# Sixteen products of constant tiles at the head of TensorE's program, in a 25,892-instruction kernel of two transformer-like blocks

## The chip, the cores and the metric

The kernel runs on one core of one Trainium2 chip. The metric is the device time of the kernel in microseconds (us), the median of the runs. Lower is better. A share of 0.2% is 3.1 us here.

## The reference, cut to what matters

Two blocks follow one another on a sequence of 512 rows of 1024 numbers in fp32. All that matters here is how the first one begins:

```python
def rms_norm(x, g, eps=1e-6):
    xf = x.astype(jnp.float32)
    y = xf * lax.rsqrt(jnp.mean(xf * xf, axis=-1, keepdims=True) + eps)
    return (y * g.astype(jnp.float32)).astype(x.dtype)
...
        h = rms_norm(x, norm_g[l])
...
            h @ w_in[l], IN_SPLITS, axis=-1)
        y_conv = conformer_conv_branch(c_glu, c_gate, conv_dw[l], conv_dw_b[l],
```

The rows are normed, multiplied by a gain, and then by `w_in` (1024 x 11264). The first branch takes 2048 of its columns, `a` and `b`, forms `a * sigmoid(b)`, and runs a causal convolution of 31 taps over the rows, channel by channel. Differential attention, cross attention to a memory of 256 rows, an output product, and a second block (gated mixing, a recurrent mixer, a feed-forward part) come after it.

## The kernel before, in words

The program of each engine is written out by hand, in order, and engines wait for each other on counted semaphores. TensorE (`pe_program`, line 1007) does everything in products of 128x128 stationary tiles. Every fp32 weight and activation is split in two fp32r parts, high and low, and each product of them is three instructions (`mm3`, lines 643 to 645: high x high, low x high, high x low). Weights come in units of 128x1024 numbers (512 KB). SyncE issues one DMA per unit into a ring of four slots (`raw`, line 751), ScalarE writes the high part (line 691), and VectorE or GpSimd the low part (line 699). The split parts have a ring of three places.

The start of the kernel, in order:

- GpSimd (`pool_program`, lines 763 to 778) sets the constants: `ident` to zero and then, as the last of them, to the identity matrix; `ones_all` to one. That last instruction (line 777) raises the semaphore `consts`. TensorE's program begins with a wait for it (line 1008).
- SyncE loads the input rows, four tiles of 128x1024 (`x_in`, line 736), the columns of gains, and then the weight units.
- ScalarE and VectorE share the sums of squares (lines 655 and 2404) and roots of the four tiles, and VectorE scales the rows (`x_in`, line 2409).
- TensorE transposes the scaled rows (`pe_turn_group`, then `pe_turn_pair`, line 979): for each of the 8 groups k of 128 features, two transposes of 128x128 for row tiles 0 and 1 (g = 0), later two for row tiles 2 and 3 (g = 1). The destinations are seven places in the matmul banks 4, 5, 6, 7, 3, 1, 2 (`row_places`), so the eighth group (k = 7) waits until the first place has been read.
- ScalarE reads each transposed group with the gain as the high part `h_T_hi` (line 654), VectorE then forms the low part `h_T_lo` (line 2390). Between those, ScalarE and VectorE split the first weight unit.
- `pe_first_unit` (line 986) computes the first unit, channel tile 0 of `b` (`conv_b` 0). It mixes the transposes of row tiles 2 and 3 with the products of rows 0 to 255, and ends with the products of rows 256 to 511, all of them with 256 moving columns. The unit has 48 instructions of `mm3`.
- `pe_conv_tile` then runs the `a` tile 0 (`conv_a` 0, 24 instructions with 512 moving columns), gate and merge units, and so on for eight tiles. When `conv_a` 0 is done, VectorE multiplies it (line 2387) and starts the taps (lines 2469 and 2390): 31 instructions per tile, back to back, into banks 4 and 5.

Bank 0 is the first place of the ring `units` (banks 0, 1, 2) and receives `conv_b` 0. TensorE works strictly in order, and `conv_b` 0 begins with an instruction that overwrites.

```python
    def pe_turn_pair(pe, what, tiles, g, pair):
...
            for n in range(2):
                if k == 0:
                    pe.wait_ge(*row_ready.at(what, 2 * g + n))
                done = pe.transpose(turned_bank(what, g, k)[:, cut(n)], tiles[2 * g + n][:, cut(k)], ident[:, :])
```

Of the kernel before, what the change touches and what calls it, by code (L numbers as in the profile page):

```python
# [14 lines left out]
P = 128  # L15
# [57 lines left out]
           "d_gate": 6144, "xq": 7168, "x_gate": 8192, "merge": 9216}  # L73
GATE_OF = {0: 0, 1: 2, 2: 1}

KEY_PAIRS = {4: ((0, 0), (0, 1)), 5: ((0, 2), (0, 3)), 7: ((1, 0), (1, 1), (1, 2), (1, 3))}


# [5 lines left out]
def unit_plan():  # L84
# [4 lines left out]
    def f(label, array, column):  # L89
        plan.append((label, array, "F", 0, column))  # L90
# [18 lines left out]
    for n in range(KT):  # L109
        f(("conv_b", n), "w_in", W_IN_AT["conv_b"] + n * P)  # L110
        f(("conv_a", n), "w_in", W_IN_AT["conv_a"] + n * P)
        for half, pair in KEY_PAIRS.get(n, ()):
            plan.append((("xk", half, pair), "w_mem_kv", "T", 256 * pair, half * 512))
# [175 lines left out]
def build(nc, dram, out):  # L289
# [40 lines left out]
    ident = usable("ident", [P, P])  # L330
    ones_all = usable("ones_all", [P, P])
# [142 lines left out]
    banks = [nc.alloc_psum_tensor(f"bank{n}", [P, 512], FP32) for n in range(8)]  # L474
# [495 lines left out]
    def pe_turn_pair(pe, what, tiles, g, pair):  # L970

        for k in (2 * pair, 2 * pair + 1):
            if k == 2 * pair or turned_last(what, k - 1) != k:
                last = turned_last(what, k)
                turn_places(what).take(pe, (what, g, last), turned_lo, what, g, last)
# [4 lines that stand above are left out]
            done.then_inc(*turned.up(what, g, k))  # L980

    def pe_turn_group(pe, what, tiles, g):
        for pair in range(KT // 2):
            pe_turn_pair(pe, what, tiles, g, pair)

    def pe_first_unit(pe, label):


        bank, (hi, lo) = unit_bank(pe, label), parts[turn_of[index[label]]]

        def products(g, k):
            tokens = turned_columns(g)
            pe.wait_ge(*turned_lo.at("x", g, k))
            return mm3(pe, bank[:, tokens], (hi[:, cut(k)], lo[:, cut(k)]), (h_T[0][:, k, tokens], h_T[1][:, k, tokens]),
                       k == 0, k == KT - 1)

        for pair in range(KT // 2):
            pe_turn_pair(pe, "x", x_in, 1, pair)
            if pair == 0:
                pe.wait_ge(*lo_ready(index[label]))  # L1000
            for k in (2 * pair, 2 * pair + 1):
                products(0, k)
        for k in range(KT):
            done = products(1, k)
        done.then_inc(*product.up(*label))

    def pe_program(pe):
        pe.wait_ge(*consts.at())
        pe_turn_group(pe, "x", x_in, 0)
        pe_first_unit(pe, ("conv_b", 0))  # L1010
        key_banks = [[], []]
        for n in range(KT):
            pe_conv_tile(pe, n, key_banks)
        pe_values(pe)
        pe_cross(pe)
        pe_differential(pe)
        pe_first_out(pe)
        pe_second_in(pe)
        pe_rwkv(pe)
        pe_second_out(pe)  # L1020
        pe_ffn(pe)
# [37 lines left out]
    def pe_conv_tile(pe, n, key_banks):  # L1059


        def mean():
            if n == 5:
                pe_conv_mean(pe, 3)

        if n:
            feature_unit(pe, ("conv_b", n), unit_bank(pe, ("conv_b", n)), h_T)
        feature_unit(pe, ("conv_a", n), unit_bank(pe, ("conv_a", n)), h_T)
        if n == 3:
            pe_turn_pair(pe, "mem", mem_in, 0, 2)  # L1070
        if n == 6:
            pe_key_turn(pe, 0)
        for half, pair in KEY_PAIRS.get(n, ()):
            pe.wait_ge(*turned_lo.at("mem", 0, 2 * pair + 1))
            pe_key_pair(pe, half, pair, key_banks[half])
        feature_unit(pe, ("conv_gate", n), unit_bank(pe, ("conv_gate", n)), h_T)
        if n in (1, 2):
            pe_turn_pair(pe, "mem", mem_in, 0, n - 1)
        feature_unit(pe, ("merge", 0, n), unit_bank(pe, ("merge", 0, n)), h_T, mid=mean)
        if n == 3:  # L1080
            pe_turn_pair(pe, "mem", mem_in, 0, 3)
        if n == KT - 1:
            pe_key_turn(pe, 1)

    def pe_values(pe):
        pe.wait_ge(*conv_done.at(KT - 2))
        for half in range(2):
            out_banks = []
            for pair in range(KT // 2):
                token_unit(pe, ("xv", half), pair, out_banks, mem_T, lambda t: value_places.take(pe, ("xv", half, t), v_lo, "x", half, t))  # L1090
                if half == 1 and pair == 1:
                    pe_conv_mean(pe, KT - 1)
                if half == 1 and pair == 2:
                    pe_conv_total(pe, "mean", stats["mean"]).then_inc(*conv_mean.up())
# [197 lines left out]
    def pe_first_out(pe):  # L1292
        for half in range(2):
            places = side if half == 0 else half_places
            out_banks = []
            for pair in range(KT // 2) if half == 0 else (0,):
                if half == 0:
                    pe.wait_ge(*y_lo.at(2 * pair + 1))
                token_unit(pe, ("w_out", half), pair, out_banks, h_T, lambda t: places.take(pe, ("w_out", half, t), row_ready, "x1", t, half))
        token_rows(pe, ("w_out", 1), out_banks, h_T, lambda: pe_turn_group(pe, "emb", x_rows, 0))  # L1300

    def pe_second_in(pe):
        first_units(pe, "emb", EARLY[0:2], h2_T)
        for n in range(2, 4):
            feature_unit(pe, ("pu", n), unit_bank(pe, ("pu", n)), h2_T)
        out_banks = []
        for pair in range(KT // 2):
            token_unit(pe, ("pv", 0), pair, out_banks, h2_T, lambda t: side.take(pe, ("pv", t), sg_gelu, t))
        head = head_features(lambda f: pe_features(pe, f), lambda f: pe_tokens(pe, f))
        for i, n in enumerate(SHIFT_ORDER):  # L1310
            feature_unit(pe, ("rwkv", n), units.take(pe, ("rwkv", n), shift_done, n), h2_T)
            if 2 <= i < 2 + TT:
                t = i - 2
                bank = side.take(pe, ("sg", t), sg_out, t)
                if t == 0:
                    pe.wait_ge(*wsp_lo.at())
                pe.wait_ge(*sg_lo.at(t))
                for g in range(4):
                    done = mm3(pe, bank[:, cut(g)], (v_sg[0][:, cut(g)], v_sg[1][:, cut(g)]),
                               (w_sp[0][:, cut(g)], w_sp[1][:, cut(g)]), True, True)  # L1320
                done.then_inc(*sg_mixed.up(t))
            head_steps(head, i, PE_HEAD_STEPS)
# [237 lines left out]
    def pe_rwkv(pe):  # L1560
        pe.wait_ge(*masks_ready.at())
        pe.wait_ge(*ident_ready.at(1))
        rwkv_rounds(lambda f: pe_features(pe, f), lambda f: pe_tokens(pe, f), lambda f: pe_chunks(pe, f),
                    lambda f: pe_states(pe, f), lambda: pe_out_steps(pe), lambda v: pe_gate_rows(pe, v))
# [21 lines left out]
    def pe_second_out(pe):  # L1586
        pe.wait_ge(*yb_lo.at(FW - 1))
        token_unit(pe, ("w_out_2", 0), KT // 2 - 1, first_out, (Mix(0), Mix(1)), None)
        out_banks = []
        token_unit(pe, ("w_out_2", 1), 0, out_banks, (Mix(0), Mix(1)),  # L1590
                   lambda t: half_places.take(pe, ("w_out_2", 1, t), moved, "mix", t, 1))
        token_rows(pe, ("w_out_2", 1), out_banks, (Mix(0), Mix(1)), lambda: pe_turn_group(pe, "ln1", x_rows, 0))
# [123 lines left out]
    def act_program(act):  # L1716
# [12 lines left out]
        for n in range(KT - 1):  # L1729
# [5 lines left out]
            if n == 6:  # L1735
                act_key_hi(act, 0)
            feed_hi(act, len(KEY_PAIRS.get(n, ())))
            if n == 5:
# [41 lines left out]
    def act_key_hi(act, half):  # L1780
        for h in (2 * half, 2 * half + 1):
            act.wait_ge(*key_turned.at(h))
            for c in range(2):
                activate(act, k_x[0][:, 2 * h + c, :], key_turned_bank(h, c), ACT.Copy, scale=column("x_kn_g", c)).then_inc(
                    *norm_hi.up("xk", h, c))
# [5 lines left out]
    def act_keys(act):  # L1791
# [25 lines left out]
        act_take(act, ("conv_b", n), conv_gate_ring.take(act, n, taken["dve"], "conv_a", n), ACT.Sigmoid)  # L1817
        feed_hi(act, 1 + len(KEY_PAIRS[n]))
        act_key_squares(act, 1)
# [1531 lines left out]
```

## Time and profile before

| what | value |
|---|---|
| three runs | 1571.91, 1572.81, 1574.12 us (median 1572.81) |
| the profiled execution | 1572.88 us |
| its span, first to last instruction | 1570.8 us |
| TensorE busy | 1518.1 us, 97% of the span |
| VectorE busy | 1093.5 us, 70% |
| ScalarE busy | 749.5 us, 48% |
| GpSimd busy | 191.9 us, 12% |
| mean granted TensorE clock, share of full | 0.995 |
| DMA | 166.18 MB, mean 106 GB/s |

The profiled execution lies 2.1 us above its span; that is what surrounds the first and the last instruction. In the timeline of the trace a row has the start (us from the first instruction), the length, the engine, the line of the code, the operation, the tiles, the shape and the count, and in brackets the idle time before it with what ended it. In the row of a group the length runs from the start of the first to the end of the last. The records of TensorE's instructions overlap: the rate of a stream is read from the distance between starts, and the length of one includes filling and emptying the array. PEld is TensorE's loading of stationary tiles.

### The profile page before, as it was taken

How to read it: one execution, taken by the hardware profiler on the slowest of the kernel's cores; microseconds unless marked ns; L12 is line 12 of the kernel's file. 1: busy time of each engine (PE TensorE's matmuls, PEld its weight loads, DVE VectorE, ACT ScalarE, POOL GpSimd, SP SyncE). 2: the span in 40 equal slices, each digit the busy share in tenths (PEclk: the TensorE clock that was granted, in tenths of full speed). 3: DMA queues.
4: the chain of work that ended last, by engine and by line, in shares of the span. 5: the costliest groups of instructions: out<-in, count | busy, mean ns of one | idle time of the engine just before them, and what ended most of it. 6: DMA issues, size and time to landing. Idle time of an engine off the chain costs nothing.

```text
span 1570.8 us, 25892 instructions
## 1 busy us (share of the span) xinstructions
PE 1518.1 (97%) x10408; PEld 1252.6 (80%) x10408; DVE 1093.5 (70%) x1898; ACT 749.5 (48%) x1253; POOL 191.9 (12%) x159
## 2 busy tenths in 40 slices
PE   7999999999999999999999999988898999999998
PEld 6878786888888877777788888767767899989886
DVE  5999994666655478758544747886547978867556
ACT  5544455535522477747632625654424544444223
POOL 2435364500010000000004000000000000000000
PEclk9999999999999999999999999999999999999999
DMA  6323243454465323232424232210002233433331
GB/s 220 94 86 120 90 147 108 160 165 146 147 184 182 116 86 95 90 111 81 147 95 142 74 121 81 81 43 4 3 29 86 90 108 106 123 97 121 101 98 54
DMA packets 45798, 166.18 MB, mean 106 GB/s; under 512 B 5280, under 2 KB 5408, under 8 KB 45680
## 3 DMA queue, kind: packets, MB, share of 16 engines
q1 hardware_dynamic: 43056, 155.95, 30.8%
q0 software_dynamic: 2624, 8.59, 1.9%
q8 instruction: 83, 1.36, 0.4%
q14 instruction: 35, 0.29, 0.1%
HBM read 162.42 MB, written 2.10 MB: 105 GB/s over the span
## 4 chain that ended last, share of the span: by engine, by line
PE 79%; DVE 15%; ACT 3%; issue 2%; DMA 0%; SPq 0%; DVEq 0%; ACTq 0%
PE bank L643 24%; PE bank L645 24%; PE bank L644 23%; DVE bank L2390 7%; PE bank L1366 1%; PE bank L1218 1%; ACT scratch L654 1%; DVE small L2416 1%; DVE x_rows L2390 1%; PE bank L1197 1%; DVE scratch L2387 0%; DVE weight_lo L699 0%; PE bank L1463 0%; ACT weight_hi L691 0%; DMA x_in<-in_x 0%
## 5 line engine op out<-in xcount | busy, mean ns | idle before, releaser
L691 ACT ACTIVATE weight_hi<-raw 128x1024 fp32r<-128x1024 f32 x195 | 205.8, 1057 | 384.6 <-PE bank L645 381.1
L643 PE MATMUL bank<-h_T_hi,weight_hi 128*128 128x512 f32 (+1 forms) x848 | 342.0, 403 | 2.8 <-DVE conv_in L2387 2.1
L699 DVE TENSOR_TENSOR weight_lo<-raw,weight_hi 128x1024 fp32r<-128x1024 f32 x138 | 168.8, 1224 | 238.6 <-ACT weight_hi L691 238.6
L645 PE MATMUL bank<-h_T_hi,weight_lo 128*128 128x512 f32 (+1 forms) x848 | 329.8, 389 | 0.0
L644 PE MATMUL bank<-h_T_lo,weight_hi 128*128 128x512 f32 (+1 forms) x848 | 329.2, 388 | 0.0
L643 PEld LDWEIGHTS bank<-h_T_hi,weight_hi 128*128 128x128 f32 x848 | 160.1, 189 | 43.2 <-issue 8.5
L2390 DVE SCALAR_TENSOR_TENSOR bank<-conv_in,columns,bank 128x512 f32<-128x512 f32 x240 | 181.4, 756 | 8.3
L644 PEld LDWEIGHTS bank<-h_T_lo,weight_hi 128*128 128x128 f32 x848 | 160.3, 189 | 33.5 <-issue 3.6
L645 PEld LDWEIGHTS bank<-h_T_hi,weight_lo 128*128 128x128 f32 x848 | 159.8, 188 | 33.8
L699 POOL TENSOR_TENSOR weight_lo<-raw,weight_hi 128x1024 fp32r<-128x1024 f32 x57 | 141.8, 2488 | 154.1 <-ACT weight_hi L691 154.1
L643 PE MATMUL bank<-h_T_hi,half_weight_hi 128*128 128x256 f32 (+1 forms) x240 | 79.1, 330 | 0.0
L644 PE MATMUL bank<-h_T_lo,half_weight_hi 128*128 128x256 f32 (+1 forms) x240 | 79.1, 330 | 0.0
L645 PE MATMUL bank<-h_T_hi,half_weight_lo 128*128 128x256 f32 (+1 forms) x240 | 79.1, 330 | 0.0
L643 PE MATMUL bank<-branch_hi,weight_hi 128*128 128x512 f32 x192 | 75.8, 395 | 0.1
L645 PE MATMUL bank<-branch_hi,weight_lo 128*128 128x512 f32 x192 | 74.8, 389 | 0.0
L644 PE MATMUL bank<-branch_lo,weight_hi 128*128 128x512 f32 x192 | 74.7, 389 | 0.0
L643 PE MATMUL bank<-weight_hi,hidden_hi 128*128 128x512 f32 x176 | 68.5, 389 | 0.0
L644 PE MATMUL bank<-weight_lo,hidden_hi 128*128 128x512 f32 x176 | 68.5, 389 | 0.0
L645 PE MATMUL bank<-weight_hi,hidden_rest 128*128 128x512 f32 x176 | 68.5, 389 | 0.0
L643 PE MATMUL bank<-weight_hi,h_T_hi 128*128 128x512 f32 x160 | 62.5, 390 | 0.0
L645 PE MATMUL bank<-weight_hi,h_T_lo 128*128 128x512 f32 x160 | 62.3, 389 | 0.0
L644 PE MATMUL bank<-weight_lo,h_T_hi 128*128 128x512 f32 x160 | 62.3, 389 | 0.0
(500 smaller groups left out, 3193.0 us busy)
## 6 DMA issues: line engine op xcount, KB each, us to landing
raw<-in_weights SPq DMA_DIRECT2D x289, 512.0 KB, 3.5
x_in<-in_x SPq DMA_DIRECT2D x4, 512.0 KB, 5.8
x_rows<-in_x POOLq DMA_DIRECT2D x4, 512.0 KB, 4.9
out<-x_rows SPq DMA_DIRECT2D x3, 512.0 KB, 2.6
mem_in<-in_mem POOLq DMA_DIRECT2D x2, 512.0 KB, 4.2
ln_rows<-in_ln_g POOLq DMA_DIRECT2D x4, 256.0 KB, 4.4
ln_rows<-in_ln_b POOLq DMA_DIRECT2D x4, 256.0 KB, 5.1
silu_row<-in_c POOLq DMA_DIRECT2D x1, 512.0 KB, 6.6
```

The source lines that it names most:

```text
L643: pe.matmul(o, lhs[0], rhs[0], start=start, stop=False, skip_group_check=onto)
L644: pe.matmul(o, lhs[0], rhs[1], start=False, stop=False, skip_group_check=onto)
L645: return pe.matmul(o, lhs[1], rhs[0], start=False, stop=stop, skip_group_check=onto)
L654: return act.activation(o, i, func, bias=bias, scale=scale)
L691: act.activation(weight_parts(u)[0][:, :], raw[u % RAW][:, :], ACT.Copy).then_inc(*weight_hi.up(u))
L699: engine.tensor_tensor(lo[:, :], raw[u % RAW][:, :], view(hi[:, :]), ALU.subtract).then_inc(*ready.up(u))
L1197: done = pe.transpose(bank[:, cut(j)], s_ring["s", h, t, 0][:, cut(j)], ident[:, :])
L1218: pe.matmul(bank, ones_head[:, :], norm_ring_d[what, h], start=True, stop=True).then_inc(*norm_sum.up(what, h))
L1366: return pe.matmul(bank[lanes, cut(m, CHUNK)], lhs(m, rows), rhs(m, rows), start=True, stop=True)
L2390: return dve.scalar_tensor_tensor(out=o, in0=a, scalar=scalar, in1=b, op0=op0, op1=op1)
L2416: dve.bn_stats(found[:, 6 * n:6 * n + 6], source[:, cut(n, 512)]).then_inc(*dve_own.up())
```

## The change

TensorE's program gets sixteen products between its wait for the constants and the first transpose. Each multiplies `ones_all` (128x128 ones, stationary) with `ident` (128 moving columns), both plain fp32, into the first 128 columns of bank 0, and each overwrites the one before. No result is read, and no semaphore is raised or waited for.

```diff
+EARLY_PRODUCTS = 16
...
     def pe_program(pe):
         pe.wait_ge(*consts.at())
+        for n in range(EARLY_PRODUCTS):
+            pe.matmul(banks[0][:, 0:P], ones_all[:, :], ident[:, :], start=True, stop=True)
         pe_turn_group(pe, "x", x_in, 0)
         pe_first_unit(pe, ("conv_b", 0))
```

## Rows read from the trace of the kernel before

**Rows 1.** The page: span, busy time by engine, chain that ended last by engine.
```profile
span 1570.8 us, 25892 instructions
...
PE 1518.1 (97%) x10408; PEld 1252.6 (80%) x10408; DVE 1093.5 (70%) x1898; ACT 749.5 (48%) x1253; POOL 191.9 (12%) x159
...
PE 79%; DVE 15%; ACT 3%; issue 2%; DMA 0%; SPq 0%; DVEq 0%; ACTq 0%
```

**Rows 2.** Timeline of all engines, 0 to 16 us.
```profile
2.34 0.28 POOL L777 TENSOR_SCALAR_AFFINE_SELECT ident<-ident 128x128 f32<-128x128 f32 x1 [0.24 <-POOL ones_head L775]
...
8.20 1.43 DVE L2409 TENSOR_SCALAR x_in<-x_in,small 128x1024 f32<-128x1024 f32 x2
...
9.09 3.63 PE L979 MATMUL bank<-ident,x_in 128*128 128x128 f32 x14 [9.09 <-DVE x_in L2409]
...
12.40 3.01 ACT L654 ACTIVATE h_T_hi<-bank,columns 128x256 fp32r<-128x256 f32 x8
...
13.53 1.54 PE L979 MATMUL bank<-ident,x_in 128*128 128x128 f32 x6 [0.81 <-DVE h_T_lo L2390]
...
14.56 1.22 DVE L699 TENSOR_TENSOR weight_lo<-raw,weight_hi 128x1024 fp32r<-128x1024 f32 x1
...
15.83 0.58 PE L643 MATMUL bank<-h_T_hi,weight_hi 128*128 128x256 f32 x1 [0.76 <-DVE weight_lo L699]
```

**Rows 3.** Timeline of TensorE, 17 to 26 us.
```profile
17.28 1.05 PE L979 MATMUL bank<-ident,x_in 128*128 128x128 f32 x4
17.98 0.56 PE L643 MATMUL bank<-h_T_hi,weight_hi 128*128 128x256 f32 x1
18.34 0.41 PE L644 MATMUL bank<-h_T_lo,weight_hi 128*128 128x256 f32 x1
18.56 0.41 PE L645 MATMUL bank<-h_T_hi,weight_lo 128*128 128x256 f32 x1
...
20.12 0.53 PE L643 MATMUL bank<-h_T_hi,weight_hi 128*128 128x256 f32 x1
20.48 0.28 PE L644 MATMUL bank<-h_T_lo,weight_hi 128*128 128x256 f32 x1
20.60 0.28 PE L645 MATMUL bank<-h_T_hi,weight_lo 128*128 128x256 f32 x1
...
25.11 0.40 PE L643 MATMUL bank<-h_T_hi,weight_hi 128*128 128x512 f32 x1
```

**Rows 4.** Waits of VectorE (25 to 245 us) and TensorE (20 to 260): total, times, longest.
```profile
DVE conv_in L2387 <- PE bank L645: 6.3, 1, 6.3
...
PE bank L1028 <- ACT conv_out L1789: 3.3, 1, 3.3
```

**Rows 5.** A plain fp32 product with ones: timeline near 634 us, and line 1213 (min/median/max ns).
```profile
633.88 1.02 PE L1213 MATMUL bank<-scratch,ones_all 128*128 128x512 f32 x2
...
L1213 PE MATMUL bank<-scratch,ones_all x16: 591/592/697, 583.2 to 781.9; 128*128 128x512 f32 x16
```

**Rows 6.** Timeline of TensorE: transposes near 880 us, and from 1213 to 1219 us.
```profile
880.05 1.86 PE L979 MATMUL bank<-ident,x_rows 128*128 128x128 f32 x15 [0.83 <-DVE x_rows L2427]
...
1213.53 0.27 PE L979 MATMUL bank<-ident,x_rows 128*128 128x128 f32 x1
1215.96 1.78 PE L979 MATMUL bank<-ident,x_rows 128*128 128x128 f32 x11 [2.16 <-DVE x_rows L2427]
1218.20 0.66 PE L979 MATMUL bank<-ident,x_rows 128*128 128x128 f32 x4 [0.47 <-DVE h_T_lo L2395]
```

**Rows 7.** Table by stretches: length, busy us of each engine, granted clock, DMA share, GB/s.
```profile
238.90:242.30 3.40, 1.07 (x5) 0.56 (x3) 3.26 (x5) 0.00 (x0) 0.00 (x0) 1.00 0.44 154
242.40:245.80 3.40, 2.50 (x10) 0.77 (x11) 1.32 (x3) 2.99 (x4) 1.62 (x1) 0.50 0.00 0
...
1109.30:1112.70 3.40, 1.57 (x56) 1.49 (x55) 0.54 (x1) 1.08 (x3) 0.00 (x0) 1.00 0.00 0
1112.80:1116.10 3.30, 3.30 (x71) 3.18 (x62) 1.31 (x2) 0.00 (x0) 0.00 (x0) 0.50 0.02 5
1213.50:1218.60 5.10, 2.34 (x18) 1.63 (x17) 4.43 (x12) 4.22 (x11) 1.74 (x4) 1.00 0.64 209
```

## The prediction

> **What bounds the kernel now.** I read the page first, then the start of the timeline, then the waits, then the table by stretches. The page says that TensorE is busy for 97% of the span and holds 79% of the chain that ended last [rows 1]. So time that TensorE loses or gains early can reach the end; the question is which time is TensorE's own.
>
> The timeline shows that before 15.83 us it isn't. The constants are ready at 2.34 + 0.28 = 2.62 us, and TensorE waits until 9.09 us for the first scaled rows. The second row tile is scaled only at 8.20 + 1.43 = 9.63 us, and only from then do the transposes stream. They don't set the pace either: ScalarE begins to read them at 12.40 us, since it splits a weight unit first, and the last six transposes wait for a bank that VectorE still reads. The first real product starts at 15.83 us, released by VectorE's low part of the first weight unit [rows 2].
>
> From 15.83 us TensorE sets the pace, at the lower of its two clock levels. Products of 256 columns start 0.22 us apart at 18.34 and 18.56 us, which is 1.2 GHz; from 20.48 us they start 0.12 us apart, which is 2.4 GHz [rows 3]. (The granted clock column has no record before 20.48 us and would print 1.00 there, so the distances have to be read.) The slow stretch is 20.48 - 15.83 = 4.65 us long, and TensorE has no gap in it. After it `conv_b` 0 ends at 25.11 us and `conv_a` 0 follows.
>
> What is won there would last. VectorE stands idle for 6.3 us until `conv_a` 0 is done, and the taps run from that point; TensorE itself waits 3.3 us near 240 us for the last of them [rows 4]. If `conv_a` 0 comes earlier, the taps and that wait move with it.
>
> **The change, part by part.**
>
> *Length of the products.* A plain fp32 product leaves two matmul records. The pair at 633.88 us takes 1.02 us, one record 0.592 us, so the second starts 1.02 - 0.592 = 0.43 us after the first, for 512 columns at 2.4 GHz [rows 5]. With 128 columns that is 0.107 us at 2.4 GHz and 0.214 us at 1.2 GHz. The transposes, which are records of the same width, show both: (1.05 - 0.41) / 3 = 0.213 us [rows 3] and (1.86 - 0.27) / 14 = 0.114 us [rows 6]. Sixteen products are 32 records: 32 x 0.214 = 6.8 us if all is slow. They start near 2.75 us and end at 9.6 us, or at 7.9 to 9.6 us if the clock rises on the way.
>
> *What they delay.* At worst the one transpose of 9.09 us goes to 9.6 us, beside VectorE's scaling of the second tile, which ends at 9.63 us [rows 2]. Cost on the path 0. Without that cover there is a second one: ScalarE reads the first transposed group at 12.40 us and takes 3.01 / 8 = 0.38 us for each, while two slow transposes take 0.43 us. The products could end at about 12.4 - 0.6 - 8 x 0.05 = 11.4 us before ScalarE notices.
>
> *Banks, queues, semaphores.* `conv_b` 0 overwrites bank 0 in order, so 0. No DMA is issued, none is moved, nothing waits for the products: SyncE, ScalarE, VectorE and GpSimd start as before. Sixteen more instructions and their tile loads are fetched by an engine that is idle for 6.4 us: 0.
>
> *The clock.* This is the only term that can be other than 0. It has two halves. First: does the clock rise on these products? In the kernel before it rose after 4.65 us without a gap, of products and eight transposes [rows 3]. 6.8 us without a gap should do it, so I expect it up by 9.6 us at the latest.
>
> Second: is it still up at 15.83 us? Between the products' end and 15.83 us TensorE has only 20 transposes. At the fast level 13 of them run from 9.68 to about 11.1 us, then the bank holds the next up to 13.53 us, six take 6 x 0.107 = 0.64 us, and TensorE idles to 15.83 us. In the 4.7 us from 11.1 us on it would be busy for 0.64 us, a seventh. Three rows are near this. The clock fell at 242.3 us after 1.07 us busy in 3.4 us, and at 1112.7 us after 1.57 us in 3.4 us. It held from 1213.5 to 1218.6 us with 2.34 us busy in 5.1 us [rows 7]. The planned stretch is thinner than both that fell. I take it that the clock falls again before or at about 15.83 us, and then has to rise as before.
>
> The bounds of this term: 0 if it has fallen, and half of the slow stretch if it holds, 4.65 / 2 = 2.3 us. A gain above 2.3 us is excluded, since only the slow stretch can shrink. If it falls shortly after 15.83 us, up to 0.3 us are won. A loss is not excluded by the rows, but needs a rise that comes later than before; since nothing that TensorE does from 15.83 us on differs, I bound it by the scatter of the rise, some 0.7 us.
>
> *A rule of the skill.* The held stretch from 1213.53 us has nothing in it but 16 transposes, and the clock stayed up [rows 6, 7]. By the Trainium skill, "TensorE: Matmul & The Clock Gate", Part 4, the clock gate doesn't count transposes as work. By that rule a stretch of transposes alone would be an idle one, the clock would be certain to fall here, and the sum would be 0. The rows at 1213 us speak against it as it stands; my 0 rests on how few transposes there are.
>
> *Sum.* 0 + 0 + 0 = 0 us, with 0 to 2.3 us of gain. Against the profiled execution (1572.88 us, 0.07 above the median of the runs) that is 1572.8 us.
>
> **The rivals.**
>
> *A. The clock holds through the transposes.* For it: the held stretch at 1213 us had gaps of 2.16 and 0.47 us [rows 6], and the gaps here would be about 2.4 and 1.6 us. Against it: 0.64 us busy in 4.7 us. It gives 1572.9 - 2.3 = 1570.6 us, a gain of 0.15%. The skill's advice to warm up with matmuls before what counts (same page, "Why this matters for your kernels") is this rival: it would give the same 2.3 us. The rows at 238.9 and 1109.3 us show that what has been warmed can be lost in one thin stretch.
>
> *B. The products run late (slower).* The place is the first transposes, the price is what passes 11.4 us. The 32 records write the same 128 columns. If each waits until the one before has left the array, it takes the full 0.41 us of a slow record [rows 3], 32 x 0.41 = 13.1 us, and they end at 15.9 us. The first product, and all behind it, comes 15.9 - 11.4 = 4.5 us later: 1577.4 us. It decides from 0.27 us a record ((11.4 - 2.75) / 32) on. Against it: products of one accumulation write the same columns at 0.22 us apart [rows 3].
>
> *C. The change doesn't do what it says.* The clock doesn't rise on products of ones and an identity matrix, or rises only for their last part. The trace has no such operands. It ends at 1572.8 us too.
>
> **How the numbers follow.** The forecast (rises, falls again) gets 0.62: two falls after busier stretches against one hold. A gets 0.25, C 0.08, B 0.05. A measurement of this kernel can tell about 0.2%, 3.1 us, from no change. The forecast, A and C all lie within that; the largest gain that the sum allows is 2.3 us, so only the scatter of the runs (2.2 us between three) can carry A beyond it: 0.05. Slower by over 3.1 us is B and some scatter: 0.04. The rest, 0.91, is no change. The range reaches from A's time less some scatter, 1570.2 us, to the highest run before plus 0.5 us, 1574.6 us; it leaves out B.
>
> **What would show it.** In the timeline of the changed kernel: 32 records with `ones_all` from about 2.75 us, 0.21 us apart and then 0.11 us; a granted clock record before 9.7 us; the first transposes at 9.6 to 9.7 us; the first product still at 15.8 us; products 0.22 us apart right after it, up to 19 to 22 us. Products 0.12 us apart at 16 us would make A right, and VectorE's wait for `conv_a` 0 would end near 28.5 instead of 30.8 us. Transposes after 11.4 us would make B right. A difference over 3.1 us in either direction would say that I have missed a mechanism.

## The result and the profile after

The changed kernel takes 1574.63 us (median of 14 runs, 1571.68 to 1577.34), the kernel before 1572.31 us in as many. The ratio is 1.0016, 95% interval 1.0009 to 1.0024: slower by 2.5 us (2.3 us between the medians), within the 3.1 us that I had called no change, but clear of noise, and above the range of the prediction by 0.03 us. The profiled execution took 1574.78 us, its span is 1572.7 us (before 1570.8 us, [rows 1]). One execution of the kernel `e9_late64` below was recorded with 5367.48 us in place of 1569 to 1575 us, and is left out of its ratio.

The page after, span and busy time, and the line of the queue q8, whose count rises when TensorE's program gets longer:

```profile
span 1572.7 us, 25955 instructions
...
PE 1523.2 (97%) x10440; PEld 1257.7 (80%) x10440; DVE 1095.5 (70%) x1898; ACT 749.8 (48%) x1253; POOL 190.6 (12%) x159
...
q8 instruction: 84, 1.38, 0.3%
```

Before, the last line reads `q8 instruction: 83, 1.36, 0.4%`. The program has 63 instructions more (32 products, 32 loads, one semaphore instruction less). 1.38 MB in 84 packets is 16 KB for each; TensorE's 21,445 recorded instructions (10,440 loads, 10,440 products, 565 of semaphores) over 84 packets are 255 in each. The 63 instructions of the change thus move TensorE's whole program behind them by a quarter of a packet.

The timeline of TensorE at the start, beside [rows 2]:

```profile
2.68 5.46 PE L1011 MATMUL bank<-ident,ones_all 128*128 128x128 f32 x32 [2.68 <-POOL ident L778]
8.61 0.33 PE L980 MATMUL bank<-ident,x_in 128*128 128x128 f32 x1 [0.47 <-DVE x_in L2412]
9.29 1.64 PE L980 MATMUL bank<-ident,x_in 128*128 128x128 f32 x13 [0.35 <-DVE x_in L2412]
13.32 1.54 PE L980 MATMUL bank<-ident,x_in 128*128 128x128 f32 x6 [2.39 <-DVE h_T_lo L2393]
15.62 0.58 PE L644 MATMUL bank<-h_T_hi,weight_hi 128*128 128x256 f32 x1 [0.76 <-DVE weight_lo L700]
```

The table by stretches for it (length, busy us of each engine, granted clock, DMA share, GB/s):

```profile
6.20:12.90 6.70, 3.91 (x32) 3.29 (x30) 5.29 (x9) 4.14 (x12) 0.00 (x0) 1.00 1.01 409
...
13.00:19.70 6.70, 5.62 (x25) 5.04 (x26) 6.37 (x14) 4.79 (x12) 1.77 (x3) 0.50 0.72 270
19.80:25.00 5.20, 5.20 (x45) 5.16 (x44) 3.47 (x6) 2.70 (x6) 0.00 (x0) 1.00 0.56 199
```

In this trace the start goes as forecast. The 32 records end at 8.1 us, the clock is up at 2.4 GHz from about 6.2 to 12.9 us, the 13 transposes run fast, then the clock is back at 1.2 GHz (0.50) and stays there until 19.7 us, past the first product at 15.62 us. The taps begin at 30.41 us, 0.43 us earlier than before. So this trace doesn't lose its 2 us at the place of the change.

VectorE's records of the two kernels pair off one to one. Their distance stays near -0.6 us up to 1050 us, swings between -2.7 and 0.3 us up to 1140 us (the clock of before falls at 1112.7 us, [rows 7], that of after doesn't), is about -1.0 us there, and is +1.67 us behind 1240 us: one instruction of the feed-forward part starts at 1242.51 us before and at 1244.18 us after. VectorE's timeline near it, before:

```profile
1242.51 0.69 DVE L2387 TENSOR_TENSOR hidden<-bank,scratch 128x512 f32<-128x512 f32 x1
```

and after:

```profile
1244.18 0.69 DVE L2390 TENSOR_TENSOR hidden<-bank,scratch 128x512 f32<-128x512 f32 x1
```

The time goes in the recurrent mixer, 1040 to 1160 us, where TensorE runs thousands of 64x64 products, and within it between 1140 and 1160 us. The chain of waits there, before (start, length, what):

```profile
1141.21 1.10 PE bank L1476 x32
...
1144.19 0.99 issue
...
1147.27 1.56 issue
1148.83 0.46 PE bank L1515 x7
1149.28 0.43 PE bank L643
...
1153.21 0.43 PE bank L643
```

and after:

```profile
1140.13 1.10 PE bank L1479 x32
...
1142.70 0.61 issue
...
1145.41 2.04 issue
1147.45 0.28 PE bank L1496 x4
...
1148.20 0.64 ACT Z L2243 x2
1148.84 0.29 ACT k_T L2246
...
1149.17 0.33 PE bank L1518 x4
1149.50 0.62 PE bank L644
...
1154.91 0.43 PE bank L644
```

"issue" is TensorE waiting for nothing that the chain shows. Before, the long one (1.56 us) falls behind the last products that ScalarE copies out (line 1495), so the copies of Z and k_T run under it. After, the long one (2.04 us) falls 32 products earlier, ahead of an instruction of line 1496 (line 1493 of before). ScalarE has to wait too, and its copies, 0.64 + 0.29 us, stand in the open. The new kernel comes in 1.08 us ahead (1140.13 against 1141.21) and leaves the wait 0.22 us behind (1149.50 against 1149.28): 1.3 us gone. Then the clock falls. The table of the two stretches around it, TensorE alone, before:

```profile
1146.20:1149.50 3.30, 1.74 (x84) 1.00 0.02 5
1149.60:1153.00 3.40, 3.40 (x28) 1.00 0.02 5
```

and after:

```profile
1146.20:1149.50 3.30, 1.14 (x40) 1.00 0.00 0
1149.60:1153.00 3.40, 3.40 (x15) 0.50 0.02 5
```

After 1.14 us of work in 3.3 us the clock went to 1.2 GHz, and by the same product the gap has grown to 1154.91 - 1153.21 = 1.7 us, 1.5 us more.

What TensorE waits for stands in the record of the queue. The two views of q8 below, of before (window 1146 to 1147.6 us) and after (1145 to 1146.1 us), hold one packet each:

```profile
q8 instruction: 1, 0.02, 4.8%
```

```profile
q8 instruction: 1, 0.02, 5.2%
```

By these records the packet of before starts at 1146.24 us and takes 1.24 us, and the wait that began at 1147.27 us ends at 1148.83 us, 1.35 us behind it. The packet of after starts at 1145.09 us and takes 0.92 us, and the wait ends at 1147.45 us, 1.44 us behind it. In the 14 traces of this document this holds for each of the 26 waits over 0.5 us in the last 256 products ahead of those of Z: each ends 1.24 to 1.55 us after a packet of q8 has landed. Where there are two, 127 or 128 products, with their loads 254 to 256 instructions, lie between them. So TensorE waits there for the next 16 KB of its program.

### The profile page after: what moved, and what is told of

Same layout as the page of the kernel before. It is cut to its first block, busy times and chain, and to the rows that moved or that the text cites. A ratio compares the mean times of both kernels' runs of the same rounds, so it can differ in the third digit from the quotient of the medians.

```text
span 1572.7 us, 25955 instructions
## 1 busy us (share of the span) xinstructions
PE 1523.2 (97%) x10440; PEld 1257.7 (80%) x10440; DVE 1095.5 (70%) x1898; ACT 749.8 (48%) x1253; POOL 190.6 (12%) x159
## 3 DMA queue, kind: packets, MB, share of 16 engines
q8 instruction: 84, 1.38, 0.3%
## 4 chain that ended last, share of the span: by engine, by line
PE 80%; DVE 14%; ACT 3%; issue 2%; DMA 0%; SPq 0%; DVEq 0%; ACTq 0%
PE bank L644 24%; PE bank L646 24%; PE bank L645 23%; DVE bank L2393 7%; PE bank L1369 2%; PE bank L1221 1%; ACT scratch L655 1%; DVE small L2419 1%; DVE x_rows L2393 1%; PE bank L1200 1%; DVE scratch L2390 0%; DVE weight_lo L700 0%; ACT weight_hi L692 0%; PE bank L1466 0%; DMA x_in<-in_x 0%
```

## The experiments

Three theories stood after this. Theory 1: what counts is where TensorE's program stands against its packets when it reaches the mixer. Theory 2: the early rise and fall of the clock costs the time. Theory 3: chance.

**Only length, no products.** In place of the products:

```diff
         pe.wait_ge(*consts.at())
+        for n in range(63):
+            pe.wait_ge(*consts.at())
```

> 63 waits on the constants that are already satisfied stand at the head of TensorE's program, and no products. The program is as much longer as with the sixteen products (63 instructions). Theory 1 (the fetch of TensorE's program in 16 KB packets, 256 instructions, falls at other places of the recurrent mixer between 1040 and 1160 us): slower than before by 1.5 to 3 us, with waits named issue at the same instructions as with the products. Theory 2 (the early clock rise and fall itself, or the shift in the phase of the clock, costs the time): same as before within 0.7 us. Theory 3 (chance of the clock in the runs taken so far): same as before.

Ratio 1.0011 (1.0002 to 1.0019). With `range(127)`:

> As e1_pad63 with 127 waits, half a packet of 256 instructions. Theory 1: the packets are fetched at yet other places, so the time differs from before by some us in either direction, and the waits named issue in the mixer move by half a packet. Theories 2 and 3: same as before within 0.7 us.

Ratio 1.0014 (1.0004 to 1.0024). With `range(191)`:

> As e1_pad63 with 191 waits, three quarters of a packet. Theory 1: another place again, and another time. Theories 2 and 3: same as before within 0.7 us, if the waits themselves end before 11.4 us.

Ratio 0.9996 (0.9986 to 1.0007). With `range(255)`:

> As e1_pad63 with 255 waits, one packet less one instruction, so the packets of the mixer begin at the instructions at which they began before. Theory 1: same as before within 0.7 us, with issue waits at the same instructions as before (near 1110 and 1147 us, 1.8 and 1.6 us), if the waits themselves end before 11.4 us; what they pass that by is added. Theory 2 and 3: same as before too.

Ratio 1.0026 (1.0015 to 1.0036). The lengths in these expectations were wrong: the traces count 31, 63, 95 and 127 more semaphore instructions, half of what was written, since two waits share an instruction. So e2_pad127 is the change's length (63) without any of its products, and it is nearly as slow (2.2 us). Its chain in the mixer is that of the change:

```profile
1144.66 2.04 issue
...
1147.45 0.64 ACT Z L2242 x2
1148.09 0.28 ACT k_T L2245
```

That speaks against theories 2 and 3: in its trace the clock is up only from 19.1 us, past the first product. e4_pad255 was no packet but half of one, and its waits took too long: TensorE's first transpose started at 16.46 us, and the taps at 34.08 instead of 30.84 us. 3.2 of its 4.1 us come from there.

```profile
16.46 3.86 PE L979 MATMUL bank<-ident,x_in 128*128 128x128 f32 x17 [16.46 <-issue]
```

At 95 and 127 instructions ScalarE's copies are in the open as well, but there is one such wait of 1.3 us between 1138 and 1156 us instead of two with 2.6 us together. The way to the first product behind them is as long as before (the table below). In e3_pad191 the clock still falls behind it, and yet the runs show no loss; that stays open.

**A whole packet.** Small products of 64x64 parts of the same constants cost four instructions each and little time:

```diff
+    def small_products(pe, count):
+        for n in range(count):
+            lanes = cut(n % 2, CHUNK)
+            pe.matmul(banks[0][lanes, 0:CHUNK], ones_all[lanes, 0:CHUNK], ident[lanes, 0:CHUNK], start=True, stop=True)
...
         pe.wait_ge(*consts.at())
+        small_products(pe, 64)
```

> 64 plain fp32 products of 64x64 parts of the same constants stand at the head of TensorE's program: 4 instructions each, 256 in all, one whole packet of the program, and the stream is as long in columns as that of the change. Theory 1 (place of the packets in the recurrent mixer): the packets begin where they began before, so same as before within 0.8 us, less what is won at the start. Theory 2 (any early activity of TensorE costs time through the clock): slower by about 2 us, as with the change.

Ratio 1.0003 (0.9992 to 1.0014): as before. (The expectation is wrong on the columns: 128 records of 64 are 8192, and the 32 of the change 4096. In time they are closer, 6.55 and 5.46 us.) In its trace the clock is up from 8.5 us and falls at 15.3 us, ahead of the first product at 16.20 us. So there is an early rise and fall, without a loss: this is what speaks against theory 2 with products at the head. Then the change itself with 48 small products behind its sixteen:

> The change as it is, its sixteen products, with 48 small ones (64x64) behind them, 256 instructions in all. They end before 11.4 us. Theory 1: same as before within 0.8 us. Theory 2: slower by about 2 us, as with the change, since the sixteen products are the same.

Ratio 0.9989 (0.9979 to 1.0000), median 1570.93 us. The same sixteen products, and no loss. It says less on theory 2 than e5_small64 does, since the clock didn't fall again (see below) and 1.7 us were won by it at the start. The long wait is back behind the last products, ahead of those of Z:

```profile
1141.81 1.49 issue
...
1145.40 1.56 issue
1146.95 0.46 PE bank L1526 x7
1147.41 0.43 PE bank L643
```

Here the products reached to 12.3 us, and the transposes followed without a gap. The clock held through the first product, and the taps began at 29.15 us, 1.7 us earlier than before. TensorE's timeline shows it:

```profile
12.33 2.84 PE L979 MATMUL bank<-ident,x_in 128*128 128x128 f32 x20
16.25 0.39 PE L643 MATMUL bank<-h_T_hi,weight_hi 128*128 128x256 f32 x1 [1.08 <-DVE weight_lo L699]
16.48 0.28 PE L644 MATMUL bank<-h_T_lo,weight_hi 128*128 128x256 f32 x1
```

**The change's length with little work**, `small_products(pe, 16)` at the head, 64 instructions:

> 16 small products (64x64) at the head: 64 instructions as with the change, about 1.7 us of TensorE at 1.2 GHz, too few to raise the clock early. Theory 1: slower than before by about 2 us, as the change. Theory 2: same as before within 0.8 us.

Ratio 1.0016 (1.0006 to 1.0027), that of the change, with its chain (1.77 us of issue, then ACT Z 0.64 and k_T 0.29 us in the open). The clock did rise early in its trace, at 12.85 us, and fell at 16.3 us; but it did the same (12.76 and 16.1 us) in the trace of e9_late64 below, which has nothing at the head and no loss.

**The clock held on purpose.** 16 products and 4 small ones at the head, 8 and 16 before the eighth transposes, 5 and 15 before the first product, 256 instructions:

> The sixteen products and 4 small ones at the head, 8 products and 16 small ones in the gap before the transposes of the eighth feature group, 5 and 15 in the gap before the first product of the first unit; 256 instructions in all, no gap of TensorE over 0.7 us between 2.7 and 15.8 us. Clock: it should stay at 2.4 GHz from its first rise on, and conv_a 0 should end 2.3 us earlier than before. Theory 1: 2.3 us faster than before, near 1570.4 us. Theory 2: no faster than before.

Ratio 0.9988 (0.9978 to 0.9998), median 1570.19 us. The clock stayed up from its first rise to 242 us, but the last gap was overfilled: the first product came at 16.92 instead of 15.83 us, and the taps began 1.05, not 2.3 us, earlier.

```profile
15.85 1.14 PE L1019 MATMUL bank<-ident,ones_all 64*64 64x64 f32 x30
16.92 0.38 PE L643 MATMUL bank<-h_T_hi,weight_hi 128*128 128x256 f32 x1
```

**Where the shift begins.** 64 instructions (8 products, 8 small) behind the mixer, in the gap of 2.16 us of [rows 6], and none at the head:

> 64 instructions (8 products and 8 small ones) stand behind the recurrent mixer, in the gap of 2.16 us near 1214 us in which TensorE waits for the scaled rows, and nothing stands at the head. Theory 1 (only the place of the packets in the mixer counts): same as before within 0.8 us, or up to 1.7 us faster where the clock would have fallen at 1217 us. Theory 1b (a shift of the program costs wherever it begins): slower by about 2 us.

Ratio 0.9999 (0.9990 to 1.0009). A shift behind the mixer costs nothing. And the change with 48 small products in the gap at 240 us of [rows 4]:

```diff
     def pe_conv_parts(pe, what, bank, tiles, ready, g):
+        if what == "mean" and g == 1:
+            pe.wait_ge(*norm_lo.at("xk", 3, 1))
+            small_products(pe, 48, banks[7])
```

> The change as it is, with 48 small products (192 instructions) in the gap of 3.3 us near 240 us in which TensorE waits for the last taps. From there on the program lies as before, one whole packet later; between 10 and 240 us it is shifted as with the change. Theory 1: not slower than before; 0 to 3 us faster, since the clock needn't fall at 242 us. Theory 2 (the early clock rise and fall) or a cost of the shift between 10 and 240 us: slower by about 2 us, less what the clock wins at 242 us. The wait named issue near 1147 us should be the 1.6 us one ahead of the product of Z, as before.

Ratio 0.9997 (0.9988 to 1.0005). The program is shifted from 10 to 240 us as with the change and whole again in the mixer. Its long wait (1.83 us) is ahead of the product of Z, as before. The ratio alone doesn't prove that the loss is gone: the clock did not fall at 242 us in its trace, and its distance from before went from +1.4 us ahead of that gap to -1.3 us behind it. But between 1140 and 1160 us, where the change lost 2.7 us, this trace lost 0.2 us. The traces of the two kernels put the loss between 240 and 1214 us.

**Versions that beat both.** 16 and 24 small at the head, 3 and 2, 5 and 2 in the two gaps, 12 products at 240 us, 256 instructions:

> All gaps of TensorE up to 15.8 us and the one at 240 us filled with products of constants, 256 instructions in all up to there: 16 products and 24 small ones at the head, 3 and 2 before the eighth transposes, 5 and 2 before the first product, 12 products at 240 us. Theory 1: as e7_hold (2.3 us at the start) and up to 3 us more at 242 us: 1567 to 1570 us. Theory 2: no faster than before.

Ratio 0.9988 (0.9978 to 0.9998), median 1569.87 us. With 8 products in the gap near 1214 us as well:

> As e11_best with 8 products in the gap near 1214 us, behind the mixer. Theory 1: as e11_best or up to 1.7 us faster, where the clock would have fallen at 1217 us. Theory 1b: slower than e11_best by about 1 us or more.

Ratio 0.9981 (0.9970 to 0.9993), median 1569.23 us. The intervals of the two overlap, so the runs don't show that the last 8 products gain anything. In its trace the wait near 1212 us shrank from 2.16 to 0.37 us, and the one near 240 us from 3.3 to 0.67 us, both under products of constants:

```profile
238.93 2.84 PE L1016 MATMUL bank<-ident,ones_all 128*128 128x128 f32 x24
242.44 1.06 PE L1049 MATMUL bank<-conv_out,ones_all 128*32 128x512 f32 x8 [0.67 <-ACT conv_out L1810]
```

The table holds all 14 traces. "Behind the wait" is the number of products between the last wait for a packet and the end of those that ScalarE copies out; "to the stage" is the time from the start of the last 256 of these products to the first instruction of line 643 behind them; "in the stage" is the time from that one to the fifth of its line, 1149.28 to 1153.21 us in before, and is longer where the clock has fallen.

| kernel | TensorE instructions ahead of the mixer | ratio to before | behind the wait | to the stage, us | in the stage, us |
|---|---|---|---|---|---|
| before | 0 | 1 | 0 | 7.1 | 3.93 |
| e1_pad63 | +31 | 1.0011 | 16 | 8.5 | 5.42 |
| the change | +63 | 1.0016 | 32 | 8.4 | 5.41 |
| e2_pad127 | +63 | 1.0014 | 32 | 8.4 | 5.42 |
| e8_small16 | +63 | 1.0016 | 32 | 8.8 | 6.56 |
| e3_pad191 | +95 | 0.9996 | 48 | 6.9 | 5.28 |
| e4_pad255 | +127 | 1.0026 (starts 3.2 us late) | 64 | 6.9 | 3.93 |
| e9_late64 | 0 | 0.9999 | 0 | 7.2 | 3.93 |
| e5, e6, e7, e10, e11, e12 | +255 | 1.0003 to 0.9981 | 0 | 6.6 to 7.6 | 3.93 to 3.96 |

The wait sits at the same place of the program in every kernel: 31, 63, 95 and 127 instructions put in ahead move it 16, 32, 48 and 64 products earlier, half their number, since each product has its load beside it, and 255 bring it back. (These kernels count 63 and 255 and not 64 and 256, since each has one semaphore instruction less than before.)

## Why the prediction was wrong

**Right, in the change's trace:** the length of the products (32 records, 5.46 us with the clock rising on the way), the transposes that they don't delay, the rise of the clock on constant operands (rival C is out), its fall at 12.9 us ahead of the first product, the first product at its old time, and with these the 0 of the clock term. Rival B did not happen: 32 records in 5.46 us are 0.17 us each. Rival A did not happen in the change's trace, and did when the gaps were thinner or filled (e6_p16s48, e7_hold). Its price, 2.3 us, was nearly right: from the first product to the taps it is 15.0 us in before and 12.9 us in e6_p16s48, e7_hold and e11_best, so 2.1 us. Of these 1.7 us reached the taps in e6_p16s48 and 2.0 us in e11_best, whose taps began at 28.88 us, since the first product came later.

The start differs between executions more than the forecast allowed for. In e10_p16gap, whose head is that of the change, the clock was up until 15.6 us, the first product came at 16.75 us and the taps at 32.23 us, 1.39 us later than before: 0.92 us of these ahead of the first product, with later rows of the input, and 0.47 us through a longer slow stretch. In e9_late64, whose head is that of before, the taps came 0.40 us earlier. What the change costs at the head on average isn't measured to better than that; the 0.7 us that I had allowed for the rise of the clock, without a row for it, cover the 0.47 us.

**Wrong:** the step "Banks, queues, semaphores", with its sentence "Sixteen more instructions and their tile loads are fetched by an engine that is idle for 6.4 us: 0." The products cost nothing where they stand. But 63 instructions put ahead of a program move everything behind them against the packets in which it is fetched, and I had looked only at the head. The term is not 0 but +2.5 us. The same length costs 2.2 us without any products (e2_pad127) and 2.5 us with 16 small ones (e8_small16), and filling it up to a whole packet takes it away (e5_small64; e6_p16s48 with the sixteen products still there). The rows for it were in the trace of before: two waits named issue, 0.99 and 1.56 us, in the stretch of 64x64 products, and a packet of q8 ahead of the end of each.

The list of rivals lacked it for the same reason. The chance of 0.91 for no change by 0.2% held because the missed term is smaller than 3.1 us, not because its causes were right; the range, 0.5 us above the highest run then known, was too narrow by 0.03 us, and the forecast itself, 1572.8 us, missed by 1.8 us and in direction.

**What is shown and what is argued.** That the position of TensorE's program in the mixer decides is shown by the runs. That the waits are waits for a program packet is shown by their place, which moves by the instructions put in, by their distance of one packet, and by the packet that lands 1.24 to 1.55 us before each ends; what happens in that time stays open. The two parts of the loss, the copies in the open and the clock that falls behind them, are in all four traces at +31 and +63: 1.3 to 1.7 us up to the stage and 1.5 to 2.6 us in it, against before. They are sizes of single traces, and how often the clock falls there over all executions isn't known: it fell near 1149 us in five of the six traces with a shifted position and in none of the eight others, but e3_pad191 has such a fall and no loss in its runs, and the medians of before differ by 1 us between sets of runs.

## What to carry to other kernels

Where TensorE runs small products without pause, as the 64x64 ones of this mixer, every instruction added or taken away ahead of it moves its program against the packets, and a wait of 1.5 to 2 us can land in the open or be hidden by chance. Before a small edit is judged by its time, run the same length of program without its work, and the edit filled up to a whole packet. Products of constants that keep TensorE's clock up pay only when they reach to the first real product without delaying it: here the sixteen of the change were over 7 us too early.

## What the runs showed of the hardware

- TensorE's program came in packets of 16 KB, 255 of its recorded instructions in each; adding 255 gave the old time back, adding 31 or 63 cost 1.7 to 2.5 us. Where it ran 64x64 products it stood still for 0.5 to 2.0 us at a packet's border, until 1.24 to 1.55 us after the packet had landed.
- The clock rises on products of ones with an identity matrix: it was up from about 6.2 us and fell at 12.9 us, after 13 transposes and in a gap of 2.39 us.
- Transposes raised the clock and kept it up. In e9_late64 TensorE did nothing before 12.76 us but transposes, from 9.34 us on, and its granted clock was up from 12.76 to 16.1 us. In e6_p16s48 TensorE did nothing but 20 transposes from 12.33 us to 16.25 us, with a gap of 1.08 us, and ran its first product at 2.4 GHz. By the Trainium skill, "TensorE: Matmul & The Clock Gate", Part 4, transposes don't count as work for the clock gate; the trace doesn't agree for these fp32 ones, as little as [rows 6, 7] did.
- A wait that is already satisfied costs TensorE time: 127 semaphore instructions kept it until 16.46 us, (16.46 - 2.68) / 127 = 0.11 us each. The small 64x64 products took 1.14 / 30 x 2 = 0.08 us for four instructions at 2.4 GHz.
